# The expert stage of a two-layer diffusion step on one Trainium2 core: plain fp32 products on 32 token columns in place of a three-product fp32r split on 128

## The reference, cut to what matters

```python
def swiglu(h, w1, w3, w2):
    return (jax.nn.silu(h @ w1) * (h @ w3)) @ w2

def moe_swiglu(h, router, w1, w3, w2):
    probs = jax.nn.softmax((h @ router).astype(F32), axis=-1)
    top_p, top_i = lax.top_k(probs, TOP_K)
    top_p = top_p / jnp.sum(top_p, axis=-1, keepdims=True)
    combine = jnp.sum(jax.nn.one_hot(top_i, N_EXPERTS, dtype=F32) * top_p[..., None], axis=-2)
    out = jnp.zeros_like(h)
    for e in range(N_EXPERTS):
        out = out + combine[..., e:e + 1].astype(h.dtype) * swiglu(h, w1[e], w3[e], w2[e])
    return out
```

## Time and profile before

| | |
|---|---|
| time, three runs | 1612.33 us median (1611.0 to 1616.38) |
| span of the profiled execution | 1608.6 us; its time apart from the span is not given, and the median is 3.7 us above it |
| first expert product to the last one's end | 638.2 to 1596.7 us of the span |
| PE busy | 1564.5 us (97%) |
| DVE, ACT busy | 1173.0 us (73%), 988.2 us (61%) |
| DMA | 498.3 MB, 310 GB/s over the span |

### The profile page before, as it was taken

The page is one execution under the profiler, slowest core; times in us unless marked ns, Lnnn a source line. Parts: engine busy times, 40 slices in busy tenths (PEclk is TensorE's granted clock), DMA queues, the critical chain, the costliest instruction groups (busy, mean ns, idle before and its releaser), DMA issues.

```text
span 1608.6 us, 23366 instructions
## 1 busy us (share of the span) xinstructions
PE 1564.5 (97%) x9115; PEld 1316.4 (82%) x9115; DVE 1173.0 (73%) x1092; ACT 988.2 (61%) x983; POOL 39.4 (2%) x39
## 2 busy tenths in 40 slices
PE   6999999999999989999999999999999999999997
PEld 4976899898789778788888888888888888888885
DVE  2465444445755856988988988988988988888987
ACT  2445333334754546867767767777777777777674
POOL 0000000000010000000000000000000000000001
PEclk9999999999999999999999999999999999999999
DMA  9498397767474044999999999999999999999993
GB/s 364 161 326 306 106 364 257 270 222 275 157 280 152 23 170 156 384 386 367 383 386 364 378 381 371 381 382 369 374 392 363 378 389 358 386 371 365 381 380 136
DMA packets 201348, 498.30 MB, mean 310 GB/s; under 512 B 8591, under 2 KB 12222, under 8 KB 186942
## 3 DMA queue, kind: packets, MB, share of 16 engines
q1 hardware_dynamic: 194030, 477.96, 80.3%
q0 software_dynamic: 3984, 14.17, 2.6%
q10 hardware_dynamic: 3264, 5.19, 0.9%
HBM read 485.60 MB, written 11.69 MB: 309 GB/s over the span
## 4 chain that ended last, share of the span: by engine, by line
PE 53%; DVE 5%; issue 4%; ACT 3%; DVEq 0%; ACTq 0%
PE banks L727 51%; DVE weights_low L2129 2%; ACT weights_high L1644 2%; PE banks L1253 2%; DVE hidden_low L2231 1%; DVE tokens_low L2142 1%; DVE arena L2227 0%; PE banks L1221 0%; ACT hT L1366 0%; DVE ring L2077 0%; ACT arena L1758 0%; DVE arena L2305 0%; DVE arena L2272 0%; ACT L1680 0%; ACT L1653 0%
## 5 line engine op out<-in xcount | busy, mean ns | idle before, releaser
L2129 DVE TENSOR_TENSOR weights_low<-pieces,weights_high 128x2048 fp32r<-128x2048 f32 x336 | 754.1, 2286 | 131.0 <-ACT weights_high L1644 131.0
L1644 ACT CAST weights_high<-pieces 128x2048 fp32r<-128x2048 f32 x336 | 624.9, 1915 | 31.0 <-PE banks L727 25.0
L727 PE MATMUL banks<-weights_high,tokens_high 128*128 128x512 f32 x896 | 354.4, 396 | 0.7 <-DVE tokens_low L2142 0.7
L727 PE MATMUL banks<-weights_high,tokens_low 128*128 128x512 f32 x896 | 349.9, 391 | 0.0
L727 PE MATMUL banks<-weights_low,tokens_high 128*128 128x512 f32 x896 | 348.6, 389 | 0.0
L727 PEld LDWEIGHTS banks<-weights_high,tokens_low 128*128 128x128 f32 x896 | 168.2, 188 | 36.0
L727 PEld LDWEIGHTS banks<-weights_high,tokens_high 128*128 128x128 f32 x896 | 168.8, 188 | 33.7 <-issue 0.8
L727 PEld LDWEIGHTS banks<-weights_low,tokens_high 128*128 128x128 f32 x896 | 168.5, 188 | 33.7
L727 PE MATMUL banks<-weights_high,hidden_high 128*128 128x512 f32 x448 | 175.9, 393 | 3.0 <-DVE hidden_low L2231 3.0
L727 PE MATMUL banks<-weights_low,hidden_high 128*128 128x512 f32 x448 | 174.5, 389 | 0.0
L1684 ACT CAST hidden_high<-banks 128x512 fp32r<-128x512 f32 x56 | 32.9, 587 | 190.7 <-PE banks L1253 190.7
(11 more groups left out here) (278 smaller groups left out, 2178.0 us busy)
## 6 DMA issues: line engine op xcount, KB each, us to landing
pieces<-in_moe_w SPq DMA_DIRECT2D x336, 1024.0 KB, 7.5
ring<-in_w_ada SPq DMA_DIRECT2D x24, 2048.0 KB, 11.8
ring<-in_ffn_w SPq DMA_DIRECT2D x15, 2048.0 KB, 11.9
ring<-in_hg_w_f SPq DMA_DIRECT2D x4, 2048.0 KB, 18.5
expert_rows<-arena POOLq DMA_DIRECT2D x9, 512.0 KB, 7.3
ring<-in_mla_w_o SPq DMA_DIRECT2D x2, 2048.0 KB, 17.8
ring<-in_hg_w_i SPq DMA_DIRECT2D x2, 2048.0 KB, 7.7
ring<-in_hg_w_q SPq DMA_DIRECT2D x2, 2048.0 KB, 7.6
```

The source lines that it names most:

```text
L727: return pe.matmul(o_, lhsT=l, rhs=r, start=start, stop=stop, skip_group_check=True)
L1644: act.copy(parts_hi[:, p % PARTS, :], raw[:, p % RAW, :]).then_inc(rounded, 1)
L2129: dve.tensor_tensor(parts_lo[:, p % PARTS, :], raw[:, p % RAW, :], parts_hi[:, p % PARTS, :].bitcast(F32), ALU.subtract).then_inc(split, 1)
```

## The change

The experts' products are made in plain fp32, from the raw pieces, with no rounding and no split: `round_piece`, `split_piece`, `tokens_low`, `hidden_low` and the `parts` tensors are gone. A pass takes CAP = 96 tokens, as three groups (TG) of 32, in place of 128; up to three rounds are provided, the later two behind the branch that runs when an expert has more than 96. The four column quarters of PE's array hold the same 32 tokens, and four blocks of weight columns pass beside one another, so that partition 32 j + i holds token i of the group for block j. Hidden columns go in three blocks of 1024 and one of 512 (SUPER). The pieces keep their size and number; a row of a w1 or w3 piece is now 1024 columns (4 KB) in three of four blocks. The memory of `parts` goes to raw pieces: 14 places, freed by PE itself (`used`). SP loads the first 14 in four steps during the recurrence's end. The output is stored by four DMAs in place of one, POOL clears 13 tiles of 128 rows in place of 9, and the last expert's rows are spread back with 24 plain fp32 products in place of 4.

```diff
@@ constants @@
-EFB = 512
-EB = E_FF // EFB
+CAP = 96
+TG = CAP // 32
+SUPER = ((0, 1024), (1024, 1024), (2048, 1024), (3072, 512))
+NSB = len(SUPER)
 PIECE = 2048
-RAW = 6
-PARTS = 6
-AHEAD = 4
+RAW = 14
+ROUNDS = -(-G * P // CAP)
...
@@ order of the pieces @@
+        PIECE_ORDER = (("w1", 0), ("w3", 0), ("w1", 1), ("w3", 1), ("w2", 0), ("w1", 2), ("w3", 2), ("w2", 1),
+                       ("w1", 3), ("w3", 3), ("w2", 2), ("w2", 3))
...
@@ SP @@
-                for p in range(AHEAD, NPC + AHEAD if e_next is not None else NPC):
-                    if p >= RAW or not isinstance(it, int) or it > 0:
-                        sp.wait_ge(split, count_at(it, NPC, p - RAW + 1))
+                for p in range(RAW, NPC + RAW if e_next is not None else NPC):
+                    sp.wait_ge(used, count_at(it, NPC, p - RAW + 1))
                     load_piece(p, e if p < NPC else e_next)
+            sp.wait_ge(g_ready, 4)
+            for p in range(2):
+                load_piece(p, 0)
             sp.wait_ge(ro_done, 8)
-            for p in range(AHEAD):
+            for p in range(2, 6):
+                load_piece(p, 0)
+            sp.wait_ge(wo_ready, 6)
+            for p in range(6, 10):
+                load_piece(p, 0)
+            sp.wait_ge(wo_ready, 8)
+            for p in range(10, RAW):
                 load_piece(p, 0)
...
@@ PE @@
+                def gate_up(kind, s):
+                    width, n = SUPER[s][1], SUPER[s][1] // 4
+                    place, nk = gate_place if kind == "w1" else up_place, PIECE // SUPER[s][1]
+                    if s:
+                        pe.wait_ge(esilu if kind == "w1" else ehid, count_at(it, NSB, s))
+                    for i in range(width // 256):
+                        w = landed_piece(first_piece[kind, s] + i)
+                        for kk in range(nk):
+                            k = nk * i + kk
+                            for t in range(TG):
+                                for j in range(4):
+                                    last = mm(place[32 * j:32 * j + 32, n * t:n * t + n], heT[:, k, 32 * t:32 * t + 32],
+                                              w[:, width * kk + n * j:width * kk + n * j + n], k == 0 and n * t % 512 == 0, k == DC - 1)
+                        last.then_inc(used, 1)
+                def down(s, parts):
...
+                            for t in range(TG):
+                                at = P * (nh * t + h) + 32 * j
+                                for jj in range(4):
+                                    last = mm(y_place[32 * jj:32 * jj + 32, 256 * t:256 * t + 256], hidT[:, s % 2, at:at + 32],
...
+                pe.wait_ge(he_ready, count_at(it, 2, 2))
+                gate_up("w1", 0)
+                gate_up("w3", 0)
+                gate_up("w1", 1)
+                turn_hidden(0)
+                gate_up("w3", 1)
+                pe.wait_ge(y_taken, count_at(it, 1, 1))
+                down(0, range(4))
+                gate_up("w1", 2)
+                turn_hidden(1)
+                gate_up("w3", 2)
+                down(1, range(4))
+                gate_up("w1", 3)
+                turn_hidden(2)
+                gate_up("w3", 3)
+                down(2, range(2))
+                turn_hidden(3)
...
+                    turn_gathered()
+                down(2, range(2, 4))
+                down(3, range(2))
...
@@ ACT @@
-            def round_piece(it, p):
...
-                act.copy(parts_hi[:, p % PARTS, :], raw[:, p % RAW, :]).then_inc(rounded, 1)
...
-            round_piece(0, 0)
-            round_piece(0, 1)
...
@@ DVE @@
-            residual(1, GATE_MIX, OUT_BANKS[1], (wo_ready, 4), {3: lambda: split_piece(0, 0)})
-            split_piece(0, 1)
+            residual(1, GATE_MIX, OUT_BANKS[1], (wo_ready, 4))
```

More of the change, by code:

```diff
@@ L482, in spent, with pieces_end, piece_at @@
                     "o": (wo_ready, 2 * j + 6)}[kind]
[L487 to L497, removed]
+        assert NPC % RAW == 0
+        PIECE_ORDER = (("w1", 0), ("w3", 0), ("w1", 1), ("w3", 1), ("w2", 0), ("w1", 2), ("w3", 2), ("w2", 1),
+                       ("w1", 3), ("w3", 3), ("w2", 2), ("w2", 3))
+        pieces = [(kind, sb, i) for kind, sb in PIECE_ORDER for i in range(SUPER[sb][1] // 256)]
+        assert len(pieces) == NPC
+        first_piece = {at[:2]: p for p, at in reversed(list(enumerate(pieces)))}
+        def pieces_end(kind, sb):
+            return first_piece[kind, sb] + SUPER[sb][1] // 256
+        BLOCKS_LANDED = [16 * sum(blocks[m][1] is not None for m in range(i, N0, RING)) if i < RING else 0 for i in range(RAW)]
+        RAW_AT = (4, 5, 0, 1, 2, 3, 6, 7, 12, 13, 8, 9, 10, 11)
+        def piece_at(p):
+            return raw[:, RAW_AT[p % RAW], :]
         TURN_LANDINGS = 16 * (NPC // RAW)
@@ L1238, in expert @@
             def expert(it, last_one=False):
[L1239 to L1253, removed]
-                    last.then_inc(ehT, 1)
[L1256 to L1288, removed]
-                    if b == 3 and not last_one:
-                        pe.wait_ge(gathered_in, count_at(it, 16, 16))
-                        turn_gathered()
-                    if b == 3 and last_one:
-                        pe.wait_ge(last_onehot, 1)
-                        for g in range(G):
-                            last = pe.transpose(bank[5][:, P * g:P * g + P], onehot[:, g, 0, :], ident)
-                        last.then_inc(last_turned, 1)
@@ L1328, in _ @@
                 turn_gathered()
[L1329 removed]
+                with pe.Fori(NE, ROUNDS * NE) as it:
                     expert(it)
@@ new lines, in take_tokens, with expert @@
+                act.copy(heT[:, 4 * half:4 * half + 4, :], place.rearrange("p (a b) -> p a b", a=4)).then_inc(he_ready, 1)
+            def expert(it, stored, last_one=False):
+                for s in range(NSB):
+                    width = SUPER[s][1] // 4 * TG
+                    act.wait_ge(used, count_at(it, NPC, pieces_end("w1", s)))
+                    if s:
+                        act.wait_ge(ehid, count_at(it, NSB, s))
+                    act.activation(e_silu[:, 0:width], gate_place[:, 0:width], ACT.Silu).then_inc(esilu, 1)
+                    if last_one and s == 2:
@@ L1716, in weigh @@
+                act.copy(y_e, y_place[:, 0:TG * 256]).then_inc(y_taken, 1)
+                act.wait_ge(y_taken, count_at(it, 1, 2))
+                rows = y_slots[0:ROUNDS * NE * CAP, :].rearrange("(i t p) (j n) -> i j p t n", t=TG, p=32, j=4)
+                for j in range(4):
+                    act.dma_start(rows[bass.ds(it, 1), j].rearrange("i p t n -> p (i t) n"),
+                                  y_e[32 * j:32 * j + 32, :].rearrange("p (t n) -> p t n", t=TG)).then_inc(y_stored, 16)
             def weigh(g, rows, landed):
@@ L2203, in slot_tables @@
                 then(last)
-                dve.tensor_tensor(onehot[:, :, 0, :], onehot[:, :, 0, :], onehot[:, :, 1, :], ALU.add).then_inc(last_onehot, 1)
+                for g in range(G):
+                    wide = last_wide[:, g, :].rearrange("p (t j n) -> p t j n", t=TG, j=4)
+                    both = (onehot[:, g, r, 0:CAP].rearrange("p (t n) -> p t n", t=TG).unsqueeze(2).broadcast_to([P, TG, 4, 32])
+                            for r in range(2))
+                    last = dve.tensor_tensor(wide, *both, ALU.add)
+                last.then_inc(last_onehot, 1)
+                for j in range(4):
+                    dve.tensor_copy(gate_cols[32 * j:32 * j + 32, :, :], gate_rows[32 * j:32 * j + 32, :, 256 * j:256 * j + 256])
             late_count = [0]
@@ new lines, in expert @@
+                for s in range(NSB):
+                    width = SUPER[s][1] // 4 * TG
+                    hidden(s)
+                    if last_one and s == 0:
+                        slot_tables()
+                    dve.wait_ge(ehT, count_at(it, NSB, s + 1))
+                    dve.tensor_copy(hidT[:, s % 2, 0:width], turn_place[:, 0:width]).then_inc(ehT_taken, 1)
+                    if last_one and s == 2:
+                        for g in range(G):
+                            mix(g, picked, 0).then_inc(mixed, 1)
```

349 lines of the change are left out of this document (148 added, 201 removed).

## The result

The changed kernel takes 1634.47 us (median of 4, 1632.61 to 1639.61), the kernel before 1612.23: a ratio of 1.0144 (95% interval 1.0122 to 1.0165). It is slower by 1.4%, and 58 us above the forecast.

A forecast was written before the change was run, and what follows sets the result against it. The prediction took PE to bound the kernel, with the DMA kept back; −45.7 (experts) + 9 (code) − 1.0 + 1.3 (ends) = −36.4 us gave 1576 us, range 1552 to 1608.

The forecast's parts named there:

- term 3: PE's expert loop: its 291 KB body must be fetched again at six returns, 1.5 us each, 9 us in all.
- terms 1 and 2: PE's experts: products 2.60 us a piece, 109.2 an expert; turns 3.2 and changes of shape 1.3 us an expert.
- Rival (c): PE's clock at its lower level, 1.2 GHz, for the expert stage: a time near 2480 us; chance 0.02.
- Rival (a): Expert pieces: column quarters overlap less well; 1617 to 1626 us with a drain (0.07), 1867 with three quarters' worth (0.06).
- Term 4: The pieces' DMA: 109.9 us an expert, under PE's 114.1, so costed at nothing.
- Terms 5 and 6: The ends: first expert product 1.0 us sooner, the work after the last product 1.3 us longer.
- (b): Code comes too late throughout, PE stopping for every block: 19 us more an expert, 1719 us; chance 0.05.
- (d): A second round, for over 96 tokens at one expert, adds 16 experts: 1826 us; chance under 0.01.
- (e): The change gives nothing, with code fetches at their upper end and pieces at 2.70 us; chance 0.04.

The follow-up runs named there:

- the light run: The changed kernel with each piece's load behind the first 14 cut to a part of its columns, PE's loop kept: 1579.8 us, one run.
- the last version: The changed kernel with PE's eight experts written out and small-product pieces spread, mostly two or three large-product pieces between two: 1570.35 us, ratio 0.9746.

## Why the prediction was wrong

**The step that failed is term 3, the code of PE's loop.** It was mis-sized: 9 us, and measured in the changed kernel 30.3 for the six stops, 6 × (33.43 − 31.08) = 14.1 for the lower clock behind them, and the gaps among the small products, where PE's "issue" between 640 and 1590 us is 54.2 in all, so 23.9 without the stops. The clock fell behind the two longest gaps also (0.84 from 1360 to 1369 us): the 161 records there take 8.61 and 8.51 us where the others take 7.20, which is 2.7 more.

```profile
1356.97 3.04 issue
1360.01 8.61 PE banks L746 x161
```

That is 71 us. Put in place of 9, the sum would have been 1576 − 9 + 71 = 1638; measured 1634.47. The 3.5 us between them are less than the 4.4 (8 × 0.55) by which terms 1 and 2 came out lower than forecast. Three things were wrong in term 3's working:

- The time that a packet takes (1.07 us in the earlier trace rows) was used for the time from asking to having. A fetch took some 6 us beside the pieces and 4 with light loads (estimates: the stops of 5.05 and 2.5 us, and the 1.4 that 50 queued instructions last). The upper bound of 4.3 us a return was therefore too low, by itself.
- That further blocks come "while earlier ones run" was reckoned with the mean of 6.4 us a block. Where products have 128 columns, 256 instructions last 256 × 2.60/192 = 3.5 us; with 50 queued ones (0.7 us) that is 2.2 short of a fetch of 6.4, and the second gaps read 1.67 to 3.04, 2.26 on average. In the other pieces a block lasts 6.9 us, and the rows of 576 records have no gap. That the next block is asked for when the one before it is begun is assumed here, and no row shows it; the light run fits (3.9 us against 4.2, no gap).
- The clock behind a stop was costed at nothing. Rival (c) had it for the whole stage or not at all.

The Trainium skill (Runtime: NRT & Kernel Launch, Instruction fetch mechanics) calls the cost of crossing from one 16 KiB block into the next mostly hidden. By that the changed kernel would have had stops at its returns and no gaps elsewhere; the trace agrees for large products and not for small ones beside a full DMA. Its rule on taken branches was cited in the prediction and held: stops where the body is 291 or 140 KB, none where it is 98. It would have been worth a rival of its own with a price above 4.3 us.

**Terms 1 and 2, right.** Twelve pieces take 31.22 us, so 2.60 each, as forecast, wherever the granted clock is 1.00. An expert without stops and gaps can be read in the last version, from 975.84 us of its chain to the end of the tokens' turn at 1088.52 + 0.87:

```profile
975.84 38.99 PE banks L749 x720
1014.82 0.92 PE banks L1292 x6
1015.74 31.22 PE banks L749 x576
1046.96 0.92 PE banks L1292 x6
1047.88 20.92 PE banks L749 x480
1068.79 0.92 PE banks L1292 x6
1069.72 18.33 PE banks L749 x432
1088.04 0.48 PE banks L1292 x3
1088.52 0.87 PE banks L1243 x8
```

113.55 us, forecast 114.1: 42 pieces at 31.22/12 are 109.27, so the turns and changes of shape are 4.28 where 4.5 and 0.4 of waits were put. Rival (a) falls: 42 waits for landings cost nothing, and the quarters run beside one another over 768 records as over 64.

**Term 4, right in its result.** PE waited for no piece's landing in any run, and 396 GB/s were to be had where 376 was feared to be all. But the sentence that landings would be far longer was wrong (7.5 us, as before), and the pieces' load had a price after all, through the code.

**Terms 5 and 6.** The first expert product begins at 638.48 us, 0.3 later than in the earlier trace rows, where 1.0 sooner was forecast; but DVE's copy at 499.90 us of before stands at 500.90 here, ahead of all that the change touches on the path, so the step itself gave 0.7. At the end, 12.9 us pass from the last product's end at 1620.62 to the span's, 11.9 before: +1.0, forecast +1.3. The copy in the timeline of DVE of before, then that of the changed kernel with the row that answers to the earlier trace rows, then the last products in the chain:

```profile
499.90 0.69 DVE L2031 COPY arena<-banks 128x512 f32<-128x512 f32 x1 [2.73 <-PE banks L727]
```

```profile
500.90 0.69 DVE L2023 COPY arena<-banks 128x512 f32<-128x512 f32 x1 [1.99 <-PE banks L746]
```

```profile
638.48 2.80 PE L746 MATMUL banks<-pieces,arena 128*32 128x256 f32 x48
```

```profile
1610.08 10.54 PE banks L746 x192
```

**Rivals.** (b), code too late throughout, was nearest: it was too late at the returns and in the four pieces of small products, not at every block. (c) is out as it was put: the granted clock is 0.97 over 760 to 1480 us, and low only behind the stops and the longest gaps. (d) and (e) are out: no second round is in the trace, and the products and turns save 119.6 − 113.55 = 6 us an expert. What the change saves is there, 40.8 us by the version without stops and with 2.7 us of gaps (1611.17 to 1570.35); in the changed kernel the code took it and 22 us more.

## What to carry to other kernels

Count the instructions of a loop's body before making its products smaller. If the body no longer stays on the chip, each return costs the time of a fetch less what is queued, so short instructions pay nearly all of it (5.05 us a return here at 27 ns an instruction, 0.67 at 114), and a clock that falls behind the stop pays again (2.35 us); writing the loop out removed that, 47 us. And in straight code, look at the stretch with the shortest instructions, not at the mean: spread it between long ones.

## What the runs showed of the hardware

- The six stops of PE of 4.87 to 5.34 us in the changed kernel were each followed by 5.4 to 6.3 us at a granted clock of 0.50 to 0.78; in the light run, two of the six stops of 2.3 to 2.8 us were followed by a row of 576 records of 32.97 us, the others by one of 31.29.
- A fetch of code is slower when the DMA engines are full: stops of 5.05 us at a DMA share of 0.96, 2.5 at 0.22.
- PE's plain fp32 products on four column quarters run at 2.60 us for 1536 columns a quarter, 1.69 ns a column, over whole experts at a granted clock of 1.00.
